# Summing the two weighted expert rows of each token on TensorE instead of VectorE, at the start of the second attention

## The reference, cut to what matters

```
for i in range(DEPTH):
    hn = rmsnorm(x, norm_mix[i])
    x = x + attention_i(hn)                       # layer 0 windowed, layer 1 differential
    x = x + hierarchical_moe(rmsnorm(x, norm_ffn[i]), ...)
return rmsnorm(x, final_norm)

# the end of hierarchical_moe: each token's two expert rows, times their weights
out = jnp.zeros_like(x2).at[slot_tok].add(ys * slot_w[:, None])
```

## Time and the profile before

| | |
|---|---|
| median of 3 runs | 2478.9 us (2478.39 to 2480.48) |
| the profiled execution, its own time | 2477.91 us |
| its span in the trace | 2476.2 us |
| TensorE matmuls busy | 2301.7 us, 93% of the span |
| VectorE busy | 1856.6 us, 75% |
| ScalarE busy | 1551.1 us, 63% |
| GpSimd busy | 277.7 us, 11% |

### The profile page before, as it was taken

How to read it: one execution, slowest core, us unless ns; L and a number is a source line. 1 busy time by engine, 2 the same in 40 slices (tenths; PEclk the granted TensorE clock), 3 DMA queues, 4 the chain that set the end, 5 groups by cost and what they waited for, 6 DMA issues and landing times. The chain is left out here.

```text
span 2476.2 us, 34758 instructions
## 1 busy us (share of the span) xinstructions
PE 2301.7 (93%) x11480; PEld 1746.2 (71%) x11480; DVE 1856.6 (75%) x2476; ACT 1551.1 (63%) x2039; POOL 277.7 (11%) x256
## 2 busy tenths in 40 slices
PE   7999999699999999949999999998969999999992
PEld 6667768577777777738888888887856777777771
DVE  6676651898889898868666667656279989888895
ACT  5565450577878777746555666554057777777772
POOL 0000030021212111030000000011001211111112
PEclk9999999799999999969999999999979999999996
DMA  4122021599999999853000000001159999999995
GB/s 128 27 75 85 26 82 40 211 384 395 404 397 403 393 401 392 346 200 94 1 26 25 25 25 25 12 30 60 46 189 368 401 394 396 396 399 396 401 384 216
DMA packets 132115, 538.62 MB, mean 218 GB/s; under 512 B 25840, under 2 KB 54640, under 8 KB 82896
## 3 DMA queue, kind: packets, MB, share of 16 engines
q1 hardware_dynamic: 113104, 470.67, 49.8%
q0 software_dynamic: 18944, 67.12, 7.7%
HBM read 487.54 MB, written 50.20 MB: 217 GB/s over the span
## 5 line engine op out<-in xcount | busy, mean ns | idle before, releaser
L1766 DVE TENSOR_TENSOR m_lo_gate<-m_raw_gate,m_hi_gate 128x2048 fp32r<-128x2048 f32 x132 | 299.1, 2289 | 75.7 <-ACT m_hi_gate L1761 72.2
L1766 DVE TENSOR_TENSOR m_lo_up<-shared,m_hi_up 128x2048 fp32r<-128x2048 f32 x128 | 292.0, 2283 | 7.1 <-ACT m_hi_up L1761 6.7
L1766 DVE TENSOR_TENSOR m_lo_down<-m_raw_down,m_hi_down 128x2048 fp32r<-128x2048 f32 x124 | 280.0, 2282 | 7.9 <-ACT m_hi_down L1761 7.9
L1761 ACT CAST m_hi_down<-m_raw_down 128x2048 fp32r<-128x2048 f32 x124 | 236.3, 1908 | 58.0 <-DMA m_raw_down<-in_moe_w_down_dram 53.7
L1761 ACT CAST m_hi_gate<-m_raw_gate 128x2048 fp32r<-128x2048 f32 x132 | 247.9, 1908 | 33.9 <-DMA m_raw_gate<-in_moe_w_gate_dram 32.0
L1761 ACT CAST m_hi_up<-shared 128x2048 fp32r<-128x2048 f32 x128 | 244.5, 1912 | 23.5 <-DMA shared<-in_moe_w_up_dram 22.6
L1897 PE MATMUL m_G<-m_hi_gate,m_x_hi 128*96 128x512 f32 x512 | 204.9, 400 | 3.8 <-DVE m_x_lo L2019 2.8
L1897 PE MATMUL m_U<-m_hi_up,m_x_hi 128*96 128x512 f32 x512 | 204.7, 400 | 0.0
L1899 PE MATMUL m_G<-m_lo_gate,m_x_hi 128*96 128x512 f32 x512 | 204.4, 399 | 0.0
L1898 PE MATMUL m_G<-m_hi_gate,m_x_lo 128*96 128x512 f32 x512 | 203.3, 397 | 0.0
L1899 PE MATMUL m_U<-m_lo_up,m_x_hi 128*96 128x512 f32 x512 | 201.9, 394 | 0.0
(11 more groups left out here) (383 smaller groups left out, 4888.2 us busy)
## 6 DMA issues: line engine op xcount, KB each, us to landing
m_raw_gate<-in_moe_w_gate_dram SPq DMA_DIRECT2D x128, 1024.0 KB, 11.6
shared<-in_moe_w_up_dram SPq DMA_DIRECT2D x128, 1024.0 KB, 12.8
m_raw_down<-in_moe_w_down_dram SPq DMA_DIRECT2D x124, 1024.0 KB, 11.9
out_rows<-m_y POOLq DMA_DIRECT2D x64, 384.0 KB, 7.5
a1n_rows<-in_diff_w_qkv_dram SPq DMA_DIRECT2D x21, 512.0 KB, 5.5
out_rows<-gain_b SPq DMA_DIRECT2D x1, 8064.0 KB, 37.9
x_res<-in_x_dram SPq DMA_DIRECT2D x8, 512.0 KB, 6.6
a0n_rows<-in_swa_w_o_dram SPq DMA_DIRECT2D x8, 512.0 KB, 3.4
```

What stands on the lines that cost most here:

```text
L1761: act.copy(self.hi[w][:, cut], self.raw[w][:, cut]).then_inc(self.hi_done[w], 1)
L1766: eng.tensor_tensor(self.lo[w][:, cut], self.raw[w][:, cut], self.hi[w][:, cut].bitcast(F32), ALU.subtract)\
```

## The change

A subclass `CombinedByTensor` replaces `Combined` in the second attention; the final norm keeps `Combined`. For each expert row VectorE writes a 128x128 diagonal matrix, the identity times the token's weight. TensorE multiplies this diagonal by the gathered row block, 128x512 at a time, in plain float32, and adds both choices up in two banks of `S`: four products per tile. VectorE then adds the two banks to `x` in one instruction. The diagonals live in `v_rows`, which holds 8 of them and therefore is no gather buffer any more: the ring has five buffers instead of six. A gather that fills a buffer again waits for TensorE's sum. Tiles 0 to 3 alternate between banks 0 and 1 and banks 2 and 3; tiles 4 to 7 all use banks 2 and 3.

```diff
+class CombinedByTensor(Combined):
+    def pair(self, tt):
+        at = 2 * (tt % 2 if tt < 4 else 1)
+        return self.banks[:, at:at + 2, :]
+
+    def gather(self, pool):
+        bufs = len(self.buffers)
+        for m in range(EARLY, 2 * NT):
+            if m >= bufs:
+                pool.wait_ge(self.combined, (m - bufs) // 2 + 1)
+            gather_back(self.t, pool, m, self.buffers[m % bufs], self.gathered[m % bufs])
+
+    def make_diagonal(self, dve, m):
+        tt, c = divmod(m, 2)
+        if m >= self.ring:
+            dve.wait_ge(self.combined, (m - self.ring) // 2 + 1)
+        dve.tensor_scalar(self.diagonals[:, m % self.ring, :], self.t.ident[:, :], self.t.weight[:, c, tt:tt + 1], None, ALU.mult)\
+           .then_inc(self.diagonal_ready, 1)
+
+    def combine(self, pe, tt):
+        bufs, out = len(self.buffers), self.pair(tt)
+        pe.wait_ge(self.diagonal_ready, 2 * tt + 2)
+        if tt >= 2:
+            pe.wait_ge(self.added, tt - 1 if tt < 4 else tt)
+        for c in range(TOP_K):
+            m = 2 * tt + c
+            pe.wait_ge(self.gathered[m % bufs], 16 * (self.base[m % bufs] + m // bufs + 1))
+            for n in range(2):
+                last = pe.matmul(out[:, n, :], self.diagonals[:, m % self.ring, :], self.buffers[m % bufs][:, n * HALF:(n + 1) * HALF],
+                                 start=(c == 0), stop=(c == TOP_K - 1))
+        last.then_inc(self.combined, 1)
+
+    def add(self, dve, tt):
+        dve.wait_ge(self.combined, tt + 1)
+        x = self.t.x[:, tt, :].rearrange("p (b n) -> p b n", b=2)
+        dve.tensor_tensor(x, self.pair(tt), x, ALU.add).then_inc(self.added, 1)
+        for m in range(self.ring + 2 * tt, min(self.ring + 2 * tt + 2, 2 * NT)):
+            self.make_diagonal(dve, m)
+
+    def complete(self, eng, tt):
+        eng.wait_ge(self.added, tt + 1)
...
         if first and o == 0:
+            if early:
+                self.norm.source.combine(pe, 0)
             for tt in range(NT - 3 if early else NT - 2):
+                if early:
+                    self.norm.source.combine(pe, tt + 1)
                 self.norm.turn(pe, tt)
...
         between = {(0, 4): NT - 3, (1, 2): NT - 2, (1, 6): NT - 1} if first and early else {}
+        combined = {(0, 2): NT - 2, (0, 6): NT - 1} if first and early else {}
         for k in ks:
+            if (o, k) in combined:
+                self.norm.source.combine(pe, combined[o, k])
             if (o, k) in between:
                 self.norm.turn(pe, between[o, k])
...
-        norm = Norm(t, "a1n", 2, sb, TO, Combined(t, "a1", (mix[:, 3, :], v_rows[:, :, :].rearrange("p a b -> p (a b)"))), lag=1)
+        source = CombinedByTensor(t, "a1", (mix[:, 3, :],), v_rows, S)
+        norm = Norm(t, "a1n", 2, sb, TO, source, lag=1)
...
+                for m in range(source.ring):
+                    source.make_diagonal(dve, m)
                 norm.vector(dve, [lambda j=j: projections.low_part(dve, 0, j) for j in range(3)], parameters)
```

More of the change, by code:

```diff
@@ L238, in complete, with __init__ @@
         eng.wait_ge(self.added, 2 * (tt + 1))
+class CombinedByTensor(Combined):
+    def __init__(self, t, name, more, diagonals, banks):
+        super().__init__(t, name, more)
+        self.diagonals, self.banks = diagonals, banks
+        self.ring = diagonals.shape[1]
+        self.diagonal_ready, self.combined = t.sem(f"{name}_diagonal_ready"), t.sem(f"{name}_combined")
+    def pair(self, tt):
[33 more added lines that the diff above has]
+        eng.wait_ge(self.added, tt + 1)
 class Norm:
```

## The result

The changed kernel took 2505.2 us (median of 4 runs, 2503.1 to 2507.25) where the kernel before took 2479.5 in the same series: a ratio of 1.0104, 95% interval 1.0092 to 1.0116. The forecast was 2506, 2496 to 2522, slower.

The account below looks back on a forecast made before the run. VectorE was taken to set the pace of the 58 us first stage. Delaying `o == 2` by 27 us, the middle of 21.3 and 32.0, made 2477.91 into 2505, plus 1 for the median: 2506 us, range 2496 to 2522.

Parts of the forecast that it names:

- The product: TensorE's diagonal products: two instructions each, 0.457 us apart at the high clock; a tile's sum readable after 3.79 us.
- The line of four: Each tile's sum, add, scaled row and transposes follow one another: 7.82 us a tile against 5.18, 7.42 without diagonals.
- The diagonals: VectorE's sixteen diagonals at 0.2 us each; first eight free in idle time, the others 0.4 us per tile.
- The start: TensorE's sum of tile 0 begins at 1.2 GHz after the first gather and ends near 1076.0 us.
- The clock: TensorE's clock may fall in each tile's pause: 21.3 us late without falls, 32 with; 27 taken, chance 0.60.
- the 21.3 us: Delay of the projection's third step, `o == 2`, with the clock high from tile 1's sum on; rival, chance 0.17.
- The sum: Projection starts 14.9 us late, `o == 2` 21.3 us late at high clock; 27 with clock falls, giving 2506 us.
- The last two tiles: Sums of tiles 6 and 7 stand inside the projection, from its start at 1115.6 to `o == 2` at 1139.5.
- The gathers: With one buffer fewer, gather 5 starts near 1076.0 instead of 1073.88 us and is just hidden, 0 to 1 us.
- the fourth rival: Five gather buffers become the wait: at most 1 to 2 us, pace-setting only under half of 9.5 + 1; no separate chance.
- Clock low throughout: Rival: TensorE's clock stays low through all six tiles ahead of the projection; 43 us late, 2522 us, chance 0.15.
- Short combine: Rival: TensorE's sum of a tile takes about 1.1 us, so the line costs less than it saves; 2469 to 2481, chance 0.05.

Follow-up runs that it names:

- e4: Changed kernel plus ten identity products on TensorE before the transposes of each of tiles 0 to 4; 2502.6 us, 1.0089 times the kernel before.
- e1: Changed kernel with TensorE issuing the sum of tile tt+2 ahead of the transposes of tile tt, same products; 2490.0 us, 1.0038 times the kernel before.
- e9: Changed kernel plus identity products before tile 0's sum, before the transposes of tiles 0 to 4 and before the projection; 2500.4 us, 1.0080 times the kernel before.
- e2: Kernel before, VectorE still summing, with only the ring cut from six gather buffers to five; 2479.9 us, 0.9996 times the kernel before.
- e6: Changed kernel with tile tt+2's sum issued ahead of tile tt's transposes and tiles 6 and 7 summed by VectorE; 2480.7 us, 1.0002 times the kernel before.
- e3: Changed kernel with each product reading only the bf16 upper halves of both operands, one instruction instead of two; 2490.7 us, 1.0042 times the kernel before.
- e7: Kernel before, but TensorE sums tiles 4 and 5, with five gather buffers and identity products in its idle time; 2481.0 us, 1.0006 times the kernel before.
- e5: Changed kernel with tiles 6 and 7 summed by VectorE's two weighted adds as before; 2494.1 us, 1.0062 times the kernel before.
- e8: Kernel before plus identity products on TensorE, 36 before tile 0's transposes and ten before those of tiles 1 to 4; 2480.8 us, 1.0007 times it.

## Why the prediction was right, point by point

The mechanism and the sum held, with errors of both signs in the terms.

- **The product.** Two instructions each, as forecast from the earlier trace rows, 0.43 us apart instead of 0.457; VectorE reads 3.6 us after the start, not 3.8.
- **The line of four.** Forecast beat 7.82, measured 7.78; without diagonals 7.42 against 7.44 (e4, adds at 1107.22 and 1114.66). The product was a little cheaper and the turn's slot a little dearer, 1.0 instead of 0.85. So the sum's match to 0.04 us owes something to two small errors that cancel. e1 shows that it is the order and not the work.
- **The diagonals.** 0.2 us each, as taken; the estimate of 0.13 us beside it was too low. The first eight cost 1.66 us in VectorE's idle time.
- **The start.** Combine 0 forecast at 5.65 us, measured from 1071.76 to the add at 1077.57, 5.8.
- **The clock.** The middle between no fall and a fall in each pause was taken, 5.7 us of 27. The prediction had the clock fall in the pauses, ahead of the turns. It fell behind two of the five, when the next combine had begun: these two took 1.7 us more each (forecast 1.8), the transposes nothing (forecast up to 1). At the projection's start, where I had assumed the high clock, it cost 1.6 us more. That is 5.0 us; the rest of e9's 5.6 is the slow start of combines 0 and 1, which the 21.3 us already held. A fall in nearly every beat, with the 32 us set beside it, did not come. The middle was a choice, not an argument, and it was met because too many falls and a forgotten place cancel: that part of the 2506 is luck.
- **The sum.** The head is 18.1 us longer than before, 14.7 without the two slow combines (forecast 14.9); the tail 7.9, of which 6.3 without the low clock (forecast 23.9 - 17.5 = 6.4). 21.0 and 5.0 make the 26.0 measured, against 21.3 and 5.7.
- **The last two tiles.** Tail forecast 1139.5 - 1115.6 = 23.9 us; measured 25.4, of which e9 gives 1.6 to the low clock.
- **The gathers.** Forecast: hidden, 0 to 1 us. TensorE never waited for one after the first, and e2 bounds the buffer's price at 1.5 us. I had taken 6.8 us to land from before; they took 5.2 here. The bound that the fourth rival gave, a beat under half of 10.5 us, fits the two runs with the shorter beat: TensorE waited for a gather for 0.94 us in e1 and 0.80 in e6.
- **The rivals.** Clock low throughout: not in the changed kernel, but up to the projection in e3, whose TensorE is less busy. Short combine: e3 tried it at the low clock only, 10 us slower. At the high clock no run has it, so the 0.05 given to it stays untested.

## What to carry to other kernels

Before work is moved from a busy engine to an idle one, write down the order in which each issues, and follow one item round: if A's step for item n + 2 stands behind its step for item n, which waits for B, which waits for A's step n + 1, the durations add and neither engine is full. The sum of such a ring can be read from the old profile, here with errors of 0.2 us in single terms. An idle engine also is not free for being idle: it needs its inputs earlier than the engine that it relieves (here by the 3.6 us of a combine), and a pause between two of its bursts may cost it its clock: in e7 one late gather did both.

## What the runs showed of the hardware that I had not expected

- GpSimd's part of a gather took up to 1.94 us in the kernel before and 0.94 to 1.01 in the changed one. The kernel before, then the changed one (count, ns min/median/max, first and last start):

```profile
L203 POOL DMA_INDIRECT shared<-out_rows,choice_slot x12: 945/1117/1941, 1065.9 to 1092.8; - x12
```

```profile
L203 POOL DMA_INDIRECT shared<-out_rows,choice_slot x13: 944/948/1010, 1067.3 to 1115.3; - x13
DMA to landing us min/median/max: 5.0/5.2/6.2
```

That VectorE mostly waits in the changed kernel is not the reason: in e1 it is busy for 22.0 of the 32 us from 1072 to 1104, and no gather took more than 1.01 us. Every gather of 1.5 us or more in before, e2, e5, e6, e7 and e8 began while VectorE was inside a weighted add or a scaled row, both `scalar_tensor_tensor` between SBUF operands (in e5 at 1089.93, 0.16 us after a scaled row's start: 1.95 us). Some that began inside one kept 0.95 (in e1 at 1096.62), so this is a coincidence in time that was not tried as a cause. The landing is earlier too, 5.2 against 6.8 us; less traffic at a time (161 against 233 GB/s) goes with it.

- Products of the identity by itself, plain float32 and 128 columns, go with a clock that stays high: with ten in each pause, the transposes behind them took 1.16 us in e4, e9 and e8, also where nothing but transposes stood between (e8, turns 1 to 4). Transposes alone ran at 1.97 us per eight in the kernel before, and so did transposes with a combine of four bf16 products between them in e3.
- The clock fell behind the same two of five like pauses in both profiles of the same program, each time within 0.4 us of the start of the combine that followed.
